# Two transformer layers' norms: halves waited for one by one, both squares on ScalarE

## The reference, cut to what matters

```python
def _rms_norm(x, g):
    xf = x.astype(jnp.float32)
    y = xf * lax.rsqrt(jnp.mean(xf * xf, axis=-1, keepdims=True) + EPS)
    return (y * g.astype(jnp.float32)).astype(x.dtype)

        x = x + _rms_norm(merged @ w_out[l], g_post_mix[l])
        h2 = _rms_norm(x, g_pre_mlp[l])
        m = jnp.square(jax.nn.relu(h2 @ w_up[l])) @ w_down[l]
        x = x + _rms_norm(m, g_post_mlp[l])
...
        x = x + mix
        x = x + swiglu(rmsnorm(x, norm_ffn[l]), ffn_w_in[l], ffn_w_out[l])
    return rmsnorm(x, norm_final)
```

## Time and profile before

| | |
|---|---|
| time, median of 3 runs | 1000.19 us (999.14 to 1001.78) |
| the profiled execution's own time | 999.15 us |
| its span | 997.4 us |
| granted clock of TensorE | 0.999 of full speed |
| busy: TensorE, VectorE, ScalarE, GpSimd | 978.0, 706.4, 474.4, 79.9 us |
| DMA | 176.35 MB, 177 GB/s in the mean |

### The profile page before, as it was taken

The page is one execution under the profiler, slowest core; times in us unless marked ns, Lnnn a source line. Parts: engine busy times, 40 slices in busy tenths (PEclk is TensorE's granted clock), DMA queues, the critical chain, the costliest instruction groups (busy, mean ns, idle before and its releaser), DMA issues.

```text
span 997.4 us, 13313 instructions
## 1 busy us (share of the span) xinstructions
PE 978.0 (98%) x5444; PEld 849.7 (85%) x5444; DVE 706.4 (71%) x745; ACT 474.4 (48%) x544; POOL 79.9 (8%) x74
## 2 busy tenths in 40 slices
PE   8999999999999999999999999999989999999997
PEld 7888888878888887999988888888888888888886
DVE  5765657877766676567677776767779977767674
ACT  5667556544533445532235443434369744434340
POOL 0400000000000001008610000000012100000000
PEclk9999999999999999999999999999999999999999
DMA  7664424655556553652224755555244647555531
GB/s 269 238 249 155 161 85 148 211 211 182 198 200 210 182 211 133 240 177 86 85 85 158 255 184 198 185 194 198 85 149 178 247 141 264 184 197 183 198 120 42
DMA packets 27292, 176.35 MB, mean 177 GB/s; under 512 B 3416, under 2 KB 3680, under 8 KB 7648
## 3 DMA queue, kind: packets, MB, share of 16 engines
q1 hardware_dynamic: 27072, 175.44, 49.9%
q10 hardware_dynamic: 160, 0.07, 0.0%
HBM read 174.45 MB, written 1.05 MB: 176 GB/s over the span
## 4 chain that ended last, share of the span: by engine, by line
PE 86%; DVE 8%; issue 2%; DMA 2%; ACT 1%; POOL 0%; POOLq 0%; DVEq 0%; ACTq 0%; SPq 0%
PE ps L1649 20%; PE ps L1622 16%; PE ps L1624 16%; PE ps L1623 16%; PE ps L1652 10%; PE ps L2026 3%; DVE wL L985 3%; PE ps L1668 1%; DMA raw<-w_stream 1%; DVE aHL L997 1%; DVE FF L1553 1%; PE ps L1806 1%; PE ps L1702 1%; DVE FF L1529 1%; PE ps L1816 1%
## 5 line engine op out<-in xcount | busy, mean ns | idle before, releaser
L985 DVE TENSOR_TENSOR wL<-raw,wH 128x2048 fp32r<-128x2048 f32 (+2 forms) x158 | 352.4, 2239 | 92.9 <-ACT wH L547 92.8
L547 ACT ACTIVATE wH<-raw 128x2048 fp32r<-128x2048 f32 (+2 forms) x158 | 292.6, 1860 | 120.4 <-PE ps L1652 55.2
L1649 PE MATMUL ps<-aHL,wH 128*128 128x512 f32 x864 | 215.8, 392 | 0.0
L1649 PEld LDWEIGHTS ps<-aHL,wH 128*128 128x128 f32 x864 | 157.2, 189 | 29.4
L1622 PE MATMUL ps<-wL,RR 128*128 128x512 f32 (+1 forms) x384 | 150.1, 391 | 0.4 <-DVE RR L997 0.4
L1623 PE MATMUL ps<-wH,RR 128*128 128x512 f32 (+1 forms) x384 | 149.2, 388 | 0.0
L1624 PE MATMUL ps<-wH,RR 128*128 128x512 f32 (+1 forms) x384 | 148.8, 388 | 0.0
L1652 PEld LDWEIGHTS ps<-aHL,wL 128*128 128x128 f32 x864 | 117.9, 190 | 8.4
L1652 PE MATMUL ps<-aHL,wL 128*128 128x256 f32 x864 | 120.5, 282 | 0.0
L1622 PE MATMUL ps<-wL,aHL 128*128 128x512 f32 (+2 forms) x296 | 119.3, 403 | 1.1 <-DVE aHL L997 0.8
L1624 PE MATMUL ps<-wH,aHL 128*128 128x512 f32 (+2 forms) x296 | 113.9, 385 | 0.0
(11 more groups left out here) (234 smaller groups left out, 1131.9 us busy)
## 6 DMA issues: line engine op xcount, KB each, us to landing
raw<-w_stream SPq DMA_DIRECT2D x152, 1024.0 KB, 4.9
raw<-w_stream SPq DMA_DIRECT2D x6, 512.0 KB, 3.5
FF<-rows_in SPq DMA_DIRECT2D x5, 512.0 KB, 8.0
raw<-w_stream SPq DMA_DIRECT2D x4, 576.0 KB, 5.3
bc<-rows_in SPq DMA_DIRECT2D x4, 512.0 KB, 8.0
xr<-x_in SPq DMA_DIRECT2D x2, 512.0 KB, 4.1
xn<-rows_in SPq DMA_DIRECT2D x1, 1024.0 KB, 4.7
out<-xn SPq DMA_DIRECT2D x4, 256.0 KB, 2.0
```

The source lines that it names most:

```text
L547: e.activation(weight_slot(i)[0][:, 0:wd], raw[:, slot, 0:wd], ACT.Copy).then_inc(hi, 1)
L985: e.tensor_tensor(l[:, 0:wd], raw[:, slot, 0:wd], h[:, 0:wd].bitcast(F32), ALU.subtract).then_inc(lo, 1)
L1649: e.matmul(ps[:, b, :], h[:, cs[k]], aHL[:, k].rearrange("p i t -> p (i t)"), start=k == 0, stop=False)
```

## The change

**TensorE, all five stages.** The wait ahead of a tile's product is cut in two: for half 0 ahead of the first weight chunk's steps, for half 1 ahead of the second's.

**Squares.** For the norms `pre_mlp`, `mix0` and `final` (WHOLE_SQUARES), ScalarE squares both halves. VectorE no longer squares there; it multiplies half 0 by the weights first, then waits for ScalarE and adds the sums. The norms `ffn0`, `mix1` and `ffn1` stay as they were.

**The last norm.** A new function `final_rows` has VectorE add a half and at once multiply it by the weights, then the other; with the power there it scales half 0 alone. ScalarE scales half 1. SyncE waits for the new semaphore `final_act` before it sends half 1.

```diff
+    WHOLE_SQUARES = ("pre_mlp", "mix0", "final")
...
             for t in range(2):
                 for c in range(2):
-                    e.wait_ge(normed, NORM["final", t, c])
+                    if c == 0:
+                        e.wait_ge(normed, NORM["final", t])
+                    else:
+                        e.wait_ge(final_act, t + 1)
                     e.dma_start(out_d[128 * t:128 * t + 128, 512 * c:512 * c + 512],
...
-                e.wait_ge(resid, RESID[name, t, 0])
-                square((name, t, 0), square_out[:, 0:512], xr[:, t, 0:512])
+                for c in range(2 if name in WHOLE_SQUARES else 1):
+                    e.wait_ge(resid, RESID[name, t, c])
+                    square((name, t, c), square_out[:, 512 * c:512 * c + 512], xr[:, t, 512 * c:512 * c + 512])
...
             for t in range(2):
                 stage_norm("final", None, t, no_wait)
+                e.wait_ge(powered, POWER["final", t])
+                e.wait_ge(final_in, 2 * t + 2)
+                e.activation(xn[:, t, 512:1024], xn[:, t, 512:1024], ACT.Copy, scale=power["final", t]).then_inc(final_act, 1)
...
+                if name in WHOLE_SQUARES:
+                    e.wait_ge(resid, RESID[name, t, 0])
+                    linked(e.tensor_tensor(half_row(xn, t, 0), half_row(xr, t, 0), gain[:, 0:512], ALU.mult))
+                    e.wait_ge(squared, SQUARE[name, t, 1])
+                    mean(name, t)
+                else:
+                    x = half_row(xr, t, 1)
...
+            def final_rows(t):
+                for c in range(2):
+                    if c == 0:
+                        e.wait_ge(first_cols, FIRST["final", t])
+                    elif t == 0:
+                        e.wait_ge(half, HALF["ffn_out1"])
+                    else:
+                        e.wait_ge(used, d_at("ffn_out1", 10) + 1)
+                    x = half_row(xr, t, c)
+                    e.tensor_tensor(x, ps[:, 2 * t + c, :], x, ALU.add).then_inc(resid, 1)
+                    e.wait_ge(resid, RESID["final", t, c])
+                    e.tensor_tensor(half_row(xn, t, c), x, bc[:, 512 * c:512 * c + 512], ALU.mult).then_inc(final_in, 1)
+                e.wait_ge(squared, SQUARE["final", t, 1])
+                mean("final", t)
+                e.wait_ge(powered, POWER["final", t])
+                e.tensor_scalar(half_row(xn, t, 0), half_row(xn, t, 0), power["final", t], None, ALU.mult
+                                ).then_inc(normed, 1)
...
-                rest(lambda: turn_rows(0))
-                flipped(name, 0)
+                rest(turn_rows)
+                flipped(name, 0, 0)
                 a_part(weights(ck[0]), 512, act, 0, 0, 0, 4, 8, 6)
+                flipped(name, 0, 1)
                 a_part(weights(ck[1]), 512, act, 0, 4, 0, late, 8, 6)
-                turn_rows(1)
+                turn_half(1, 0)
+                turn_half(1, 1)
                 a_part(held(ck[1]), 512, act, 0, 4, late, 4, 8, 6).then_inc(half, 1)
-                flipped(name, 1)
+                flipped(name, 1, 0)
                 a_part(held(ck[0]), 512, act, 1, 0, 0, 4, 8, 7).then_inc(used, 1)
+                flipped(name, 1, 1)
                 a_part(held(ck[1]), 512, act, 1, 4, 0, 4, 8, 7).then_inc(used, 1)
```

More of the change, by code:

```diff
@@ L144, in program @@
     FLIP_LO = numbered(*[k for k in FLIP if k[0] not in ("mq", "mk", "lq")])
-    NORM = numbered(*[(s, t, c) for s in ("mix",) + STAGES + ("final",) for t in (0, 1) for c in (0, 1)])
+    NORM = numbered(*[(s, t, c) for s in ("mix",) + STAGES for t in (0, 1) for c in (0, 1)], ("final", 0), ("final", 1))
     def norm_order(*ends):
@@ L151, in program @@
     LAT = [("lat", n) for n in range(4)]
-    keys = [key for key in norm_order((0,), (1,)) if key[2] == 0 or key[0].startswith("post")]
+    WHOLE_SQUARES = ("pre_mlp", "mix0", "final")
+    keys = [key for key in norm_order((0,), (1,)) if key[2] == 0 or key[0].startswith("post") or key[0] in WHOLE_SQUARES]
     SQUARE = numbered(*keys[0:2], ("mix", 1, 1), *LAT, *keys[2:])
@@ L257, in program @@
         bound_act, bound_dve = sem("bound_act"), sem("bound_dve")
+        final_in, final_act = sem("final_in"), sem("final_act")
         ac_zero, hg_sig, hg_in, leveled, hg_q, hg_k, gathered = (
@@ L1013, in norm_rows @@
             def norm_rows(name, t, gain):
[L1015 to L1022, removed]
+                if name in WHOLE_SQUARES:
[5 more added lines that the diff above has]
+                    x = half_row(xr, t, 1)
+                    e.wait_ge(resid, RESID[name, t, 1])
+                    linked(e.scalar_tensor_tensor(square_out[:, 512:1024], x, 1.0 / 1024, x, ALU.mult, ALU.mult,
+                                                  accum_out=sum_sq[name, t, 1]))
+                    settle()
+                    e.wait_ge(squared, SQUARE[name, t, 0])
+                    mean(name, t)
+                    linked(e.tensor_tensor(half_row(xn, t, 0), half_row(xr, t, 0), gain[:, 0:512], ALU.mult))
                 settle()
@@ L1607, in _ @@
             for t in range(2):
-                stage_rows("final", t, out_done_wait("ffn_out1", 10))
-                norm_rows("final", t, bc)
+                final_rows(t)
         @block.tensor
@@ L1922, in stage, with turn_half, turn_rows @@
                 ck = a_at(*first)
[L1924 to L1929, removed]
-                rest(lambda: turn_rows(0))
-                flipped(name, 0)
+                def turn_half(t, g):
+                    e.wait_ge(normed, NORM[name, t, g])
+                    if t:
+                        flipped(name, 0, g)
+                    flips(xn_rows(t, g), 4, 4 + g)
+                def turn_rows():
+                    turn_half(0, 0)
+                    turn_half(0, 1)
+                rest(turn_rows)
+                flipped(name, 0, 0)
                 a_part(weights(ck[0]), 512, act, 0, 0, 0, 4, 8, 6)
+                flipped(name, 0, 1)
                 a_part(weights(ck[1]), 512, act, 0, 4, 0, late, 8, 6)
-                turn_rows(1)
+                turn_half(1, 0)
+                turn_half(1, 1)
                 a_part(held(ck[1]), 512, act, 0, 4, late, 4, 8, 6).then_inc(half, 1)
-                flipped(name, 1)
+                flipped(name, 1, 0)
                 a_part(held(ck[0]), 512, act, 1, 0, 0, 4, 8, 7).then_inc(used, 1)
+                flipped(name, 1, 1)
                 a_part(held(ck[1]), 512, act, 1, 4, 0, 4, 8, 7).then_inc(used, 1)
```

## The result

The changed kernel takes **996.84 us** (median of 17 runs, 995.95 to 999.26), the kernel before in 17 runs taken with them 1000.77 us: ratio 0.9966, 95% interval 0.9958 to 0.9974, so 2.6 to 4.2 us less (3.4 by the ratio). The forecast was 996.5. The profiled execution of the changed kernel took 995.95 us with a span of 994.2; the one of before 999.15 with 997.4. Trace against trace the change is worth 3.2 us, and the sum had 3.7.

The account below looks back on a forecast made before the run. TensorE, busy 98% of the span, was taken as the bound, so only its gaps and the tail could shrink: 2.14 + 1.06 + 0 + 0.5 = 3.7 us off 1000.19 gave 996.5 us, range 995.2 to 998.7.

Parts of the forecast that it names:

- the sum: All predicted terms together: 2.14 + 1.06 + 0 + 0.5 = 3.7 us saved.
- pre_mlp and mix0, 2.14 us: Tile 1 in both stages: earlier rows and split waits let TensorE restart at 203.84, not 204.91, 1.07 us each.
- the power's 0.55: GpSimd's power in pre_mlp and mix0 takes 0.55 us, not 0.92, with no VectorE multiplication beside it.
- The rival that kept the power at 0.92: pre_mlp and mix0 give only 0.62 us each, the tail 0.1; 2.4 us in all, 997.8 us; chance 0.13.
- ffn0 and ffn1, 1.06 us: Split waits close TensorE's gap before tile 1's product whole, 0.53 us in each stage, and both arrive.
- The rival of more absorption: A ScalarE and VectorE chain absorbs the ffn0 and ffn1 gains too; 2.6 us in all, 997.5 us; chance 0.15.
- mix1, 0 us: mix1's 0.53 us is lost to longer waiting at TensorE's later 1.91 us gap; counted 0, bounds 0 and 0.53.
- the gap at 741.87 grows by about 0.5: Sign of a right prediction: TensorE's 1.91 us idle there, waiting for VectorE's convolution inputs, lengthens by about 0.5 us.
- The tail, 0.5 us: Last norm: last output transfer issued 0.67 us sooner, transfers may push each other by up to 0.26; 0.41 to 0.67.
- The waits for aHL: TensorE's waits for low halves of turned rows sink from 2.5 us to 0.3 to 0.6, left in pre_mlp and mix0.
- The slower rival: Tile 0 of pre_mlp and mix0: a late weight load delays ScalarE's copy of turned rows; 1000.4 us; chance 0.05.
- The base: Time the saving was taken from: the median of 1000.19 us, 1.0 us over the profiled execution.

Follow-up runs that it names:

- the fourth experiment: Changed kernel with VectorE's multiplication of half 0 put back behind the mean, beside GpSimd's power, in pre_mlp and mix0: 998.06 us against 1000.15, ratio 0.9975.
- mix1 unsplit: Changed kernel with token tile 1's wait in mix1 taken at once for both halves again: 996.92 us against 999.74, ratio 0.9972.
- waits alone: Kernel before with only TensorE's waits for turned halves taken one by one in all five stages: 998.28 us against 1000.15, ratio 0.9975.
- the mixer's gap filled: Changed kernel with six matmuls of identity by identity between the first two groups of gates of the recurrent mixer: 996.77 us against 999.74, ratio 0.9973.
- the repeat: Changed kernel, unaltered, measured and traced once more beside the combined kernels: 996.63 us against 1000.49, ratio 0.9968.
- more matmuls at the start: Changed kernel with eight more matmuls of zeros in TensorE's two gaps at the start: 996.15 us against 999.74, ratio 0.9968.
- the last norm alone: Kernel before with only the last norm changed: 999.9 us against 1000.15, ratio 0.9994.
- the earlier split: Changed kernel with ScalarE's weight split ahead of its copies of tile 1's turned rows in mix1: 995.34 us against 999.74; second time 995.62 against 1000.44.
- the squares alone: Kernel before with only ScalarE squaring both halves and VectorE multiplying ahead of the mean in pre_mlp and mix0: 999.54 us against 1000.15, ratio 0.9992.

## Why the prediction came out as it did

- **pre_mlp and mix0, 2.14 us: right** (1.03 + 1.02 = 2.05). The mean, the power's 0.55 and the restart are as worked out; the 0.04 us by which the restart came later than forecast (203.88, not 203.84) is what is missing in each stage. The rival that kept the power at 0.92 falls with the fourth experiment.
- **ffn0 and ffn1, 1.06 us: right** (0.51 and 0.50). The rival of more absorption falls: nothing behind them takes it up in any trace without added matmuls.
- **mix1, 0 us: within the bounds, but too low, and the place was wrong.** Its 0.52 us entered the mixer, and it was the first gap there that grew, from 0.34 to 0.57 us (734.01), while the later one stayed at 1.91: "the gap at 741.87 grows by about 0.5" is wrong. With the fall in both traces nothing of it got through (mix1 unsplit). In the traces without the fall part of it did: 0.14 us (waits alone), 0.28 (the multiplication put back), 0.29 (the mixer's gap filled), 0.34 (the repeat) and 0.48 (more matmuls at the start). The kernel with the last norm alone, which has no such term, gained 0.13 there by chance. So the term is nearer to 0.3 us than to 0; the bounds, 0 and 0.53, held.
- **The clock in the mixer: the step that failed.** The sum had no term for it, since the trace of before has 1.00 throughout. The fall took 1.5 us of TensorE's ledger at once (2.84 to 1.35), and the waits behind it gave 0.9 back: 0.4 to 0.6 us stay, by the two pairs of executions of one kernel (0.64 for the changed one; 1.09 - 0.66 = 0.43 for the one with the earlier split). Four of the fourteen traces have it (the changed kernel's first, the squares alone, mix1 unsplit, the second of the earlier split), and of the two kernels traced twice each had it once. So the change doesn't bring it about by itself; whether it makes it likelier is open, since before has a single trace, without it. Without the fall the change would be worth 3.6 to 3.8 us in the traces. That the sum's 3.7 lies there is partly luck: mix1's term was some 0.3 too low, and the other terms together 0.2 too high.
- **The tail, 0.5 us: right in kind, 0.42 in size**, near the lower bound. The last issue came 0.72 us sooner, where 0.67 was forecast; the landing took 0.29 us more, where the sum allowed up to 0.26 and counted 0.17. The two transfers start 0.37 us apart, in before 0.66, and only the second one lands later, as the prediction feared. ScalarE's scaling took 0.72 us and not 0.63, since I had priced a scaling by the row of a square, but that cost nothing: it ends at 991.26, ahead of the issue at 991.43, as the prediction said. An estimate by the figure that the Trainium skill gives ("ScalarE: Activation LUTs", section "Rules for kernel authors") comes to 0.72 us for 512 elements, and the row agrees with it.
- **The waits for aHL** were to sink to 0.3 to 0.6 us and are gone from the list. In pre_mlp the restart at 203.88 still comes 0.30 us behind the free slot (the third matmul started at 203.35, and they follow each other every 0.23), so the halves still decide there. The list, which goes by idle time, no longer counts it: the idle time before that matmul is 0.14 us.
- **The slower rival** did not come: ScalarE's copies in tile 0 gave TensorE no wait.
- **The base.** The forecast took the median of three runs, 1000.19; with 17 it is 1000.77, and 5 of the changed kernel's 17 runs are at the mean clock of 0.994. Both medians hang on how many such runs they hold, each some 2 us longer, which is about as much as the largest term of the sum. The medians differ by 3.9 us, the ratio says 3.4 and the traces 3.2: that the forecast of 996.5 lies 0.3 us from the median is therefore closer than the sum deserves, with a base 0.6 us too low and a fall that it didn't have.

## What to carry to other kernels

Split a wait by what the first instructions behind it need, and count the gain once per place where the engine then stood, by starts and not by the idle column; look behind it for the first gap whose releaser does not hang on that engine, since it can take up part of the gain or all of it (of mix1's 0.53 us, 0 to 0.48 arrived). Small GpSimd steps on a critical chain belong where VectorE has nothing to run on two SBUF operands, or ahead of it: moving one multiplication of 0.68 us was worth 0.4 us, twice. And where a change is worth under 0.5% of the span, compare traces instruction by instruction and give the granted clock of every run: here chance differences of 0.6 and 2 us between runs of one kernel stood beside terms of 0.4 to 1 us.

## What had not been expected of the hardware

- TensorE's granted clock fell to 1.2 GHz for 3 us in the mixer in some executions of one kernel and not in others (the changed kernel: yes and no; the one with the earlier split: no and yes), each time behind a gap of 1.9 to 2.0 us, and in other traces not at all behind the same gap. It fell at the start for nearly 7 us (0.50 in the whole window of 8 to 14 us) in four traces, behind gaps of 0.8 to 1.1 us; the mean clock of 0.994 that points to it had 8 of 25 runs of the changed kernel, and none of 18 once matmuls were added in the gaps there.
- At the start the column of the granted clock reads 1.00 while ten 128x128 passes take 2.50 us; in the execution above the same passes took 1.38 us at 6.30. The column doesn't show the lower level there; the durations do.
- A fetch of 0.02 MB of instructions beside a load of 1024 KB went with 1.0 to 1.7 us more for the load, and it came there in each of the four kernels with matmuls added (eight at the start, 800 us earlier, six in the mixer, or both).
